# Start of a two-block transformer kernel: first loads issued by two engines, norm sums by token, parameter steps moved ahead of the norm, angles in quarters

## What is computed

```python
shift1, scale1, gate1, shift2, scale2, gate2 = jnp.split(silu(c) @ ada_w[0] + ada_b[0], 6, axis=-1)
h = rms_norm(x, norm1_g) * (1 + scale1) + shift1
# s5_mixer: 64 groups of 16 channels, a 64-dim complex diagonal state each
dt = exp(log_dt); mag = exp(lr * dt); ab = mag * (cos(li * dt), sin(li * dt))
f = (ab - 1) / (lr + i li); bb = f * b
state_t = ab * state_(t-1) + bb @ u_t;   y = Re(c @ state) + d * h
g = gelu(y);   x = x + gate1 * g * sigmoid(g @ w_glu + b_glu)
```

## Time and profile before

| | us |
|---|---|
| three runs, median | 2476.98 (2474.41 to 2478.2) |
| the profiled execution | 2477.59 |
| its span, first to last instruction | 2475.8 |
| PE busy in the span | 2287.5 (92%) |
| DVE / ACT / POOL busy | 1066.9 / 843.8 / 39.7 |
| mean granted TensorE clock | 0.962 |

### The profile page before, as it was taken

The page is one execution under the profiler, slowest core; times in us unless marked ns, Lnnn a source line. Parts: engine busy times, 40 slices in busy tenths (PEclk is TensorE's granted clock), DMA queues, the critical chain, the costliest instruction groups (busy, mean ns, idle before and its releaser), DMA issues.

```text
span 2475.8 us, 29368 instructions
## 1 busy us (share of the span) xinstructions
PE 2287.5 (92%) x11126; PEld 1741.5 (70%) x11126; DVE 1066.9 (43%) x1591; ACT 843.8 (34%) x1288; POOL 39.7 (2%) x29
## 2 busy tenths in 40 slices
PE   4588899999998789999999999998999998999997
PEld 2354667777866556888888766666888876888885
DVE  4685343323346664534334344444433334333332
ACT  4332332222235464433223344333222223222222
POOL 3200000000000000000000000000000000000000
PEclk9698899999999899999999999989999999999998
DMA  6589545545422003233233211111333322332331
GB/s 187 192 272 306 199 136 181 179 149 186 141 76 69 9 18 95 71 109 104 83 106 115 70 51 52 51 40 47 88 100 93 93 85 68 93 111 85 94 106 55
DMA packets 360892, 269.98 MB, mean 109 GB/s; under 512 B 20402, under 2 KB 346400, under 8 KB 350544
## 3 DMA queue, kind: packets, MB, share of 16 engines
q1 hardware_dynamic: 346928, 256.37, 33.8%
q10 hardware_dynamic: 13856, 12.13, 1.9%
HBM read 265.39 MB, written 3.08 MB: 108 GB/s over the span
## 4 chain that ended last, share of the span: by engine, by line
PE 80%; DVE 7%; ACT 4%; DVEq 2%; issue 2%; DMA 2%; POOLq 2%; ACTq 1%; SPq 0%; POOL 0%
PE G L482 58%; PE G L1921 8%; PE AD L394 2%; DVE tb L562 1%; PE MS L1257 1%; PE MS L2150 1%; PE X L2131 1%; PE X L2397 1%; ACT whi L462 1%; PE X L1663 1%; DVE wlo L468 1%; DVEq L561 1%; PE X L1627 1%; DMA TTall<-blocks 0%; PE G L1123 0%
## 5 line engine op out<-in xcount | busy, mean ns | idle before, releaser
L468 DVE TENSOR_TENSOR wlo<-raw,whi 128x1024 fp32r<-128x1024 f32 (+1 forms) x296 | 380.8, 1287 | 1010.0 <-ACT whi L462 1009.0
L462 ACT ACTIVATE whi<-raw 128x1024 fp32r<-128x1024 f32 (+1 forms) x296 | 328.1, 1108 | 940.7 <-PE G L482 778.7
L482 PE MATMUL G<-Ahi,whi 128*128 128x512 f32 x1440 | 574.8, 399 | 17.0 <-DVE Alo L567 9.7
L482 PE MATMUL G<-Ahi,wlo 128*128 128x512 f32 x1440 | 563.6, 391 | 0.0
L482 PE MATMUL G<-Alo,whi 128*128 128x512 f32 x1440 | 563.6, 391 | 0.0
L482 PEld LDWEIGHTS G<-Ahi,whi 128*128 128x128 f32 x1440 | 272.3, 189 | 99.2 <-issue 30.6
L482 PEld LDWEIGHTS G<-Ahi,wlo 128*128 128x128 f32 x1440 | 272.6, 189 | 58.2 <-issue 3.4
L482 PEld LDWEIGHTS G<-Alo,whi 128*128 128x128 f32 x1440 | 272.2, 189 | 57.8
L482 PE MATMUL G<-mhi,whi 128*128 128x512 f32 x528 | 212.0, 402 | 0.0
L482 PE MATMUL G<-mlo,whi 128*128 128x512 f32 x528 | 205.7, 390 | 0.0
L482 PE MATMUL G<-mhi,wlo 128*128 128x512 f32 x528 | 205.5, 389 | 0.0
(11 more groups left out here) (503 smaller groups left out, 2673.1 us busy)
## 6 DMA issues: line engine op xcount, KB each, us to landing
ada_s<-in_ada_w SPq DMA_DIRECT2D x48, 1024.0 KB, 7.5
raw<-in_w_in SPq DMA_DIRECT2D x64, 512.0 KB, 4.1
ada_ff<-in_w_ada SPq DMA_DIRECT2D x24, 1024.0 KB, 6.1
raw<-in_ffn_w_gate SPq DMA_DIRECT2D x44, 512.0 KB, 3.9
raw<-in_ffn_w_up SPq DMA_DIRECT2D x44, 512.0 KB, 3.9
raw<-in_ffn_w_down SPq DMA_DIRECT2D x32, 704.0 KB, 4.7
raw<-in_w_ffn_in SPq DMA_DIRECT2D x44, 512.0 KB, 3.9
raw<-in_w_ffn_out SPq DMA_DIRECT2D x16, 704.0 KB, 4.7
```

Source lines behind the costliest of these rows:

```text
L462: last = E.eng.activation(whi[j][:, k0:k0 + k, 0:c], raw[j][:, k0:k0 + k, 0:c], ACT.Copy)
L468: last = E.eng.tensor_tensor(wlo[j][:, k0:k0 + k, 0:c], raw[j][:, k0:k0 + k, 0:c], whi[j][:, k0:k0 + k, 0:c].bitcast(FP32), ALU.subtract)
L482: mm = E.eng.matmul(out_, a[j][:, k0 + kk, 0:c], b(kk), start=first and kk == 0 and n == 0, stop=last and kk == k - 1 and n == 2)
```

## The change

SP's and ACT's queues share the first loads: ACT issues x first, then every second small vector, then ada slices 0 to 3; SP issues the log-dt vector, the constants, the other vectors, C, B, slices 4 to 7, positions. Slices 4 to 7 have buffers of their own (two new ones, two in hS), so none of the eight waits. The norm's sums are taken by tokens: ACT squares xn rows with an accumulator, takes the root of four columns, scales the identity by it and PE spreads it with ones. The copies of C move from DVE to ACT. The multiples come from two broadcast instructions. Angles are made in quarters in buffers of their own; quarter 0 on ACT before the norm, quarter 1 after it, quarters 2 and 3 in loop iterations 0 and 1. The rotary angles move behind the norm on DVE, their sines into iteration 1 on ACT, the rest into iteration 2. inputs_dve(1) and powers_dve(1) move behind the norm. The core of the diff, in the order of the file (the last hunks are those of `s5_dve` and `scan_dve`, `s5_act`, and ACT's list):

```diff
         def load_early(E, s):
-            if s >= NEARLY:
-                E.eng.wait_ge(S("early_done"), s - NEARLY + 1)
+            if s >= KD:
+                E.eng.wait_ge(S("early_done"), s - (KD if s < KD + NEARLY else NEARLY) + 1)
...
+        def start_sp(E):
+            d(con[:, :], A["consts"][:, 0:C_ALL]).then_inc(S("dma_con"), 16)
+            load_vectors(E, 0)
...
+            for s in range(4, 8):
+                load_early(E, s)
...
+        def loads_act(E):
+            E.eng.dma_start(xn, A["x"][0].rearrange("(a p) d -> p a d", p=P)).then_inc(S("dma_x"), 16)
+            load_vectors(E, 1)
+            for s in range(4):
+                load_early(E, s)
...
         def params_act(E):
             E.eng.activation(Pi[:, :, :], tt9, ACT.Sin)
+            E.eng.drain().then_inc(S("s5_act"), 1)
+            E.eng.wait_ge(S("ct_done"), E.nth("ct_done"))
...
+                        E.eng.activation(c[a * NST:(a + 1) * NST, 16 * q:16 * q + 16, :], src[:, :, a, :], ACT.Copy)
+            E.eng.drain().then_inc(S("c_taken"), 1)
+        def token_rms_act(E):
+            log_exp(E)
+            a.drain()
+            for b in range(4):
+                a.activation(squares, xn[:, b, :], ACT.Square, accum_out=oms0[:, b:b + 1])
+                a.drain()
+            tiny_root(E, oms0[:, :], oms0[:, :], 1.0 / D)
+            a.drain()
+            a.wait_ge(S("sq_free"), E.nth("sq_free"))
+            for b in range(4):
+                e = a.activation(sq[0][:, b * P:(b + 1) * P], ident, ACT.Copy, scale=oms0[:, b:b + 1])
+            e.then_inc(S("sq_ready"), 1)
...
+            a.activation(rstd[:, :], MS[:, :], ACT.Copy).then_inc(S("ms_done"), 1)
+        def token_rms_pe(E):
+            for b in range(4):
+                mm = E.eng.matmul(MS[:, b * P:(b + 1) * P], ones, sq[0][:, b * P:(b + 1) * P], start=True, stop=True)
...
         def params_dve(E):
-            reduce_angle(E, rang[:, 0, :, :], rang[:, 1, :, :])
...
-            for n in range(RB + 1):
-                v.tensor_scalar(xt9[:, :, n], p["x"], float(n), None, ALU.mult)
-                v.tensor_scalar(tt9[:, :, n], p["th"], float(n), None, ALU.mult)
+            each(E, (tt9, p["th"].unsqueeze(2).to_broadcast(sh), steps, ALU.mult),
+                 (xt9, p["x"].unsqueeze(2).to_broadcast(sh), steps, ALU.mult))
...
-                        v.tensor_copy(c[a * NST:(a + 1) * NST, 16 * q:16 * q + 16, :], src[:, :, a, :])
-            v.drain().then_inc(S("c_taken"), 1)
             inputs_dve(E, 0)
+            E.eng.wait_ge(S("c_taken"), 1)
             powers_dve(E, 0)
-            inputs_dve(E, 1)
-            powers_dve(E, 1)
             ada_take(E, 0)
             gain_scale(E, acol[:, :], V_N1, mod[0][:, 8:16], 0)
             rms_dve(E)
             norm_dve(E, xk, col(acol, 0), col(mod[0], 0), lambda k: hS[:, k, :], None)
+            inputs_dve(E, 1)
+            powers_dve(E, 1)
+            rope_angles_dve(E)
...
         def params_pe(E):
+            x_turn_pe(E)
+            E.eng.matmul(AD[:, :], ident, con[:, 0:512], start=True, stop=True)
+            E.eng.wait_ge(S("silu_c"), 1)
+            for s in range(2):
+                early_slice(E, s)
...
             mm.then_inc(S("ct_done"), 1)
-            x_turn_pe(E)
-            rms_pe(E)
-            E.eng.wait_ge(S("silu_c"), 1)
-            E.eng.matmul(AD[:, :], ident, con[:, 0:512], start=True, stop=True)
-            for s in range(4):
+            for s in range(2, 4):
                 early_slice(E, s)
+            token_rms_pe(E)
+            for s in range(4, 8):
+                early_slice(E, s)
+            ada_turn(E, 0)
             E.eng.wait_ge(S("c_taken"), 1)
             turn_inputs_pe(E, 0)
             E.eng.wait_ge(S("ms_done"), E.ahead("ms_done", 1))
             kernel_pe(E, 0)
-            for s in range(4, 8):
-                early_slice(E, s)
-            ada_turn(E, 0)
...
         def angles_pool(E):
-            for h in range(2):
+            for q in range(4):
+                if q > 0:
+                    E.eng.wait_ge(S("trig"), q)
...
+                if k < 2:
+                    angles_act(E, k + 2)
+                if k == 1:
+                    rope_trig_act(E)
+                    preset(E, ACT.Gelu_apprx_tanh)
...
-                        E.eng.wait_ge(S("trig"), 2)
+                        E.eng.wait_ge(S("ms_done"), 2)
+                if k == 2:
+                    rope_trig_dve(E)
...
-            E.eng.wait_ge(S("cosine"), h + 1)
+            E.eng.wait_ge(S("cosine"), k // 2 + 1)
...
-            rms_act(E, xk)
-            angles_act(E)
-            inputs_act(E, 0)
-            kernel_act(E, 0)
-            ada_evict(E, 0)
-            norm_act(E, col(mod[0], 0), lambda k: hS[:, k, :], between={0: lambda: turn_steps_act(E, 0)})
-            preset(E, ACT.Gelu_apprx_tanh)
+            token_rms_act(E)
+            angles_act(E, 0)
+            ada_evict(E, 0)
+            inputs_act(E, 0)
+            norm_act(E, col(mod[0], 0), lambda k: hS[:, k, :],
+                     between={0: lambda: turn_steps_act(E, 0), 1: lambda: kernel_act(E, 0)})
+            angles_act(E, 1)
             s5_act(E)
```

More of the change, by code:

```diff
@@ L161, in program @@
         Wst = [[sb(f"Wst{k}{i}", [P, 4, P], where=s5a) for i in range(2)] for k in range(2)]
+        ada_first = [sb(f"ada_first{i}", [P, 2 * D], where=s5a) for i in range(2)]
         s5a.close()
@@ L211, in program @@
         CA.append([CA2[:, i, :].rearrange("p (a b c) -> p a b c", a=4, c=NCH) for i in range(2)])
-        ang_x = CA2[:, :, :].rearrange("p a b -> p (a b)")[:, 0:16 * NB]
+        squares = CA2[:, :, :].rearrange("p a b -> p (a b)")[:, 0:D]
         Ust = [sb(f"Ust{k}", [P, 8, NB], where=s5) for k in range(2)]
@@ L222, in program @@
         scan = sb("scan", [P, 5, 4 * NB], where=s5)
+        ang = sb("ang", [P, 3, 8 * NB], where=s5)
+        oms0 = sb("oms0", [P, 4], where=s5)
+        ada_s5 += ada_first + [hS[:, 4 * i:4 * i + 4, :].rearrange("p a b -> p (a b)") for i in range(2)]
         Braw = [TTall[:, 0, 512 * i:512 * i + 512].rearrange("p (a b) -> p a b", b=NCH) for i in range(2)]
@@ L712, in params_act, with rope_trig_dve @@
             E.eng.drain().then_inc(S("s5_act"), 1)
+        def rope_trig_dve(E):
+            E.eng.wait_ge(S("s5_act"), E.nth("s5_act"))
+            each(E, (trig[:, 0, :, :], trig[:, 0, :, :], trig[:, 0, :, :], ALU.mult))
+            E.eng.tensor_scalar(trig[:, 0, :, :], trig[:, 0, :, :], -2.0, 1.0, ALU.mult, ALU.add)
         def params_dve(E):
@@ L835, in angles_pool, with angles_act @@
                 p.drain().then_inc(S("ang"), 1)
-        def angles_act(E):
+        def angles_act(E, q):
             a = E.eng
-            for h in range(2):
-                cs, sn = turns[h]
-                E.eng.wait_ge(S("ang"), E.nth("ang"))
-                a.activation(cs, ang_x, ACT.Sin, scale=0.5)
-                a.activation(sn, ang_x, ACT.Sin)
-                a.drain().then_inc(S("trig"), 1)
-                a.activation(cs, cs, ACT.Square)
-                a.drain()
-                a.activation(cs, cs, ACT.Identity, scale=-2.0, bias=con[:, C_ONE:C_ONE + 1])
-                a.drain().then_inc(S("cosine"), 1)
+            cs, sn = [t[:, (q % 2) * 512:(q % 2 + 1) * 512] for t in turns[q // 2]]
+            E.eng.wait_ge(S("ang"), E.nth("ang"))
+            a.activation(cs, ang[:, 0, :], ACT.Sin, scale=0.5)
+            a.activation(sn, ang[:, 0, :], ACT.Sin)
+            a.drain().then_inc(S("trig"), 1)
+            a.activation(cs, cs, ACT.Square)
+            a.drain()
+            a.activation(cs, cs, ACT.Identity, scale=-2.0, bias=con[:, C_ONE:C_ONE + 1])
+            a.drain().then_inc(S("cosine"), 1)
         def flat(t):
@@ L1182, in early_sp @@
         def early_sp(E):
-            for s in range(4, 44):
+            for s in range(8, 44):
                 load_early(E, s)
```

101 lines of the change are left out of this document (58 added, 43 removed).

## The result

| | before | after |
|---|---|---|
| median of 5 runs each, us | 2478.2 (2474.41 to 2484.91) | 2463.72 (2462.1 to 2467.53) |
| ratio, with its 95% interval | | 0.9942 (0.9923 to 0.996) |
| profiled execution; its span | 2477.59; 2475.8 | 2462.1; 2460.3 |
| mean granted clock | 0.962 | 0.963 |

A forecast was written before the change was run, and what follows sets the result against it. Bound: the chain from late vectors through POOL's two angle halves and ACT's list to the norm. 39.8 us earlier, 29.2 at scan 0, less 2.4, 2.3 and 0.5, leaves 24.0: median 2453, range 2441 to 2465 (own 2445 to 2460).

The forecast's parts named there:

- the take: DVE taking the norm's shift and scale after ada evict and turn: forecast at 46.3 in place of 86.1, 39.8 us earlier.
- rival 1: Iteration 0 and before: DVE and POOL collide harder, 9 us per quarter, ACT's extra uncovered; gain 14, time 2463; chance 0.14.
- Rival 4: Long stretch from 300 us: PE's granted clock falls, 0.016 costing 33 us, time 2486; chance 0.05.
- rival 3: Start and loop: vectors land at 7.5, POOL and DVE hardly meet, ACT covered; gain 36, time 2441; chance 0.12.
- First loads: Kernel start, loads over two queues: last small vectors at 11.05 as before, gain 0, bounds +3.5 and -3 us.
- C transposed 28.4: Before the norm: PE, after x, one ones-matmul, two slices and sixteen transposes of C, done at 28.4.
- iteration 0: First loop iteration, beside POOL's quarter 3: DVE's 15.2 us plus 4 makes 19.2 against 16.8, 2.4 us given back.
- the ring: The loop's cycle of waits through DVE and PE, taken as 16.8 us before for iteration 0.
- Iteration 1: Second loop iteration: ACT gets 4.6 us more, 2.3 covered, so 2.3 us given back, bounds 0 and 7.
- rival 2: End of the loop set by transfers: half the gain lost gives 2465, all lost 2477; chance 0.09.
- the GLU: First matmul of the layer's GLU, behind the loop: forecast 24.0 us earlier.
- signs named beforehand for "wrong": Last vector after 14; ct_done wait over 3 us; slow DVE in iteration 0; longer last iterations; long-stretch clock not 0.98.

The follow-up runs named there:

- the last run: Changed kernel with vectors ahead of x, slices behind B and C, C first on PE, rotary part late, POOL ahead in own buffers: 2454.55 us, ratio 0.9914.

## Why the prediction was right and wrong

**Right: the mechanism and its largest term.** ACT's list was the bound, and the change takes POOL's serial halves out of it; with the quarters put back ahead of the take it comes at 89.8. That the time is almost the 2463 of rival 1 is a coincidence. Rival 4 did not come (clock 0.98 over the long stretch, as before), nor did rival 3 (the vectors came late, not at 7.5, and POOL and DVE did collide). A quarter of POOL's work costs DVE 4.1 and 4.3 us, forecast 4; rival 1's 9 did not come. The norm took 11.3 us (forecast 12.4, a term that the text gives without its working), and from its end to scan 0 it was 15.5 (forecast 14.9).

**Wrong: the sizes on the way to the take, 7.2 us of the missing 8.5.** The prediction's step "First loads" took 11.05 for the vectors, gain 0, with bounds of +3.5 and -3. It was 14.41, at the bound on the bad side: +3.4. The text itself had the second half behind x and said 11 to 13 for it, and then took the low end; the run with the vectors ahead of x (9.60) shows that this was their cause. Next, "C transposed 28.4" was 33.6, 5.2 late, of which 1.8 are new. There PE's work was costed and B's arrival was not: the sum looked at the slices' rate and never asked what they do to the 1 MB of B and C in the other queue. The runs showed the wait in its place, 17.8 to 19.8 us to land for three of the four loads beside the slices and 7.9 to 9.9 without them. The split of the 5.2 is one of book-keeping: the chain of after runs through B alone, and the vectors' 3.4 lie inside the wait for it. PE could have begun with C at 28.2, 3.5 later than the forecast's 24.7, had B been there; with the vectors early and B late, nothing was gained. Copies of C were 0.38 each, 3.1 in all, forecast 2.7: +0.4. Third, the token sums, forecast 9.4 from the copies of C to the end of rstd, took 11.4: +2.0, of which 1.35 are PE's short matmuls, 2.05 for 0.7 (the text's own terms up to 39.2 add to 39.0). The rest up to the take (sines, evict, turn) came out 0.4 shorter. Together 3.4 + 1.8 + 0.4 + 2.0 - 0.4, the whole 7.2.

**Wrong: iteration 0, 1.5 us.** It gave back 3.9, forecast 2.4. The 19.2 forecast for DVE's own work beside POOL became 20.7 from scan to scan; without POOL it is 16.4, so the addition of 4.3 was right, and the base was too small: I had reckoned 15.2 us of DVE work with no waits where the ring, without POOL, takes 16.4. Iteration 1 gave back 2.0 (forecast 2.3), but that the two agree is in part luck. The forecast put it all on ACT's extra work. Without the rotary sines iteration 1 took 19.4 us, and in the last run, without quarter 3's sines there too, 19.3, still 1.1 above the 18.2 of before. What is left lies on PE:

```profile
110.25 1.89 PE L408 MATMUL AD<-ada_s,cact 128*1 128x512 f32 x8 [2.46 <-DVEq L470]
112.07 1.98 PE L1173 MATMUL X<-Ust,Wst 128*64 128x64 f32 x32
```

These took 1.04 and 1.71 before; the granted clock was 0.50 from 110 to 114 us in that run and 0.73 from 135 to 138 before. From scan 2 to scan 7 the loop gained 1.3 where 0.5 was to be lost.

**Behind the loop: 2.2 us, not rival 2.** From scan 7 to the GLU it took 33.5 us before and 35.7 after. PE's wait for the last Toeplitz block grew from 4.23 to 6.55. The rows of after, then of before, then of the run with all quarters before the norm:

```profile
223.20 1.12 PE L1199 MATMUL G<-CA,Sst 64*64 64x128 f32 x8 [6.55 <-DMA TTall<-blocks]
...
238.47 1.88 PE L408 MATMUL AD<-ada_s,cact 128*1 128x512 f32 x8 [2.80 <-DMA ada_s<-in_ada_w]
```
```profile
238.90 1.12 PE L1123 MATMUL G<-CA,Sst 64*64 64x128 f32 x8 [4.23 <-DMA TTall<-blocks]
```
```profile
250.15 1.12 PE L1197 MATMUL G<-CA,Sst 64*64 64x128 f32 x8 [6.20 <-DMA TTall<-blocks]
```

The waits for the last slices stayed (2.98 and 1.57 before, 1.81 and 2.80 after). Rival 2 would have it that a loop which comes earlier waits longer at its end. But the third kernel's scan 7 lies 9.5 us later than before, and it too took 36.0 us from there to the GLU; all executions of changed kernels took 35.1 to 36.8, wherever their loop lay. So the 2.2 us do not come from the loop being early. The forecast's argument against rival 2, that the backlog moves with the last iterations, held. In part they mirror the 1.3 gained in the loop: from scan 2 to the GLU it is 124.0 before and 124.9 after, with 124.1 to 126.3 in the other runs, so 0.9 is lost in all, little beside that spread. What in the changed kernels lengthens the Toeplitz wait stays open; no run took that transfer apart.

The sum of the parts: 24.0 - 7.2 + 0.5 (take to scan 0) - 1.5 + 0.3 + 1.8 - 2.2 - 0.1 (behind the GLU) = 15.6, the span's 15.5. Of the signs named beforehand for "wrong", two came and both told the truth: the last small vector after 14 (14.4), and ACT waiting for `ct_done` for over 3 us (3.54). The landmarks named for "right" all missed their 5 us: POOL's quarters began at 50.7, 65.9 and 83.3 for 42, 60 and 76, ada_turn(0) at 52.9 for 45, scan 0 at 80.3 for 74, and scan 2 came 16.6 earlier for 25.

## What to carry to other kernels

When loads are spread over two queues, list for each queue what lies behind the large transfer and what the other queue is streaming at that time; small or short-packet loads that something waits for go ahead of both. When a change removes one wait from a chain, look at each input of the next steps for its own arrival time, since several late inputs hide each other, and mending one alone can gain nothing. Work on an engine that slows another beside it is costed per piece (here 4 us of DVE for each of POOL's quarters), wherever it is put beside a busy DVE. Before a landmark of one trace is read to 1 us, look how far it moves between executions in which nothing ahead of it differs.

## What the runs showed of the hardware

- An issue can block its engine. The four issues of B and C (256 KB each, in the order issued) took SP 0.43, 2.34, 0.58 and 3.17 us before; 0.41, 1.16, 13.33 and 5.49 in after, with x and four slices in the other queue; and 0.41, 1.53, 4.52 and 4.28 with the slices behind them. It is not free to have short-packet loads in a queue whose engine has more to issue.
- POOL slows DVE unevenly. Two-input operations of 512 columns, 0.68 us alone, took 1.09 to 1.76 beside POOL, and between those another one took 0.68. The Trainium skill ("GPSIMD Engine Reference", Specifications) names DVE instructions with two SBUF inputs as a case of contention between the two engines; these rows agree. They are not the only ones slowed: a TENSOR_SCALAR of 32 columns with one input took 1.09 at 31.9 in after, with POOL at work, and 0.18 before, without it.
- PE's clock in the start is low at times and costs on the chain. After 9.1 us without work PE ran at a granted clock of 0.50 (45 to 48 us), the lower of its two levels, 1.2 GHz, and four 128-column matmuls took 2.05 us. The first eight transposes of C took 1.06 us at 30.9 in after and 1.92 at 31.0 in the run with sums by channels (granted clock 0.75 and 0.50 from 30 to 34 us), so a landmark can differ by 1 us between executions for this alone, and by 2 between the extremes.
